# A third mixer whose keys, queries, values and gates load activations instead of weights, with norms, rotation and state output by token

## What is computed

```python
q, k, v, z, xbc, dt_raw = split(h @ w_in, [1024, 2048, 3072, 4096, 6144])   # h = rms_norm(x)
attn = dilated_attention(q, k, v, positions, g_q, g_k)     # 16 heads of 64
ssm = ssd_mixer(z, xbc, dt_raw, ...)                       # 16 heads of 64, state 128, 4 groups
x = x + concat(rms_norm(attn), ssm) @ w_out
```

## Time and profile before

| | us |
|---|---|
| median of three runs | 3288.57 (3285.89 to 3290.23) |
| profiled execution, its own time | 3288.93 |
| its span in the profile | 3287.0 |
| TensorE busy | 3270.5 (99%), 16658 matmuls |
| VectorE, ScalarE, POOL busy | 2215.1 (67%), 1524.6 (46%), 188.7 (6%) |
| third mixer, from its first weight matmul to its last state product | 2014.8 to 2369.7, 354.9 |

### The profile page before, as it was taken

The page is one execution under the profiler, slowest core; times in us unless marked ns, Lnnn a source line. Parts: engine busy times, 40 slices in busy tenths (PEclk is TensorE's granted clock), DMA queues, the critical chain, the costliest instruction groups (busy, mean ns, idle before and its releaser), DMA issues.

```text
span 3287.0 us, 41280 instructions
## 1 busy us (share of the span) xinstructions
PE 3270.5 (99%) x16658; PEld 2778.4 (85%) x16658; DVE 2215.1 (67%) x1898; ACT 1524.6 (46%) x1520; POOL 188.7 (6%) x272
## 2 busy tenths in 40 slices
PE   8999999999999999999999999999999999999999
PEld 7888888888888888888888888999989888888887
DVE  6565777777676665777777766577776566665565
ACT  6645434444445654444444345347554533333333
POOL 0100000000000000000000000001030000000000
PEclk9999999999999999999999999999999999999999
DMA  7456777777755446877777764434454455555554
GB/s 281 155 179 223 267 261 254 248 255 251 259 195 206 161 166 208 278 251 260 253 247 254 256 215 158 167 130 145 139 205 152 168 192 191 191 191 191 191 191 166
DMA packets 106523, 686.29 MB, mean 209 GB/s; under 512 B 14064, under 2 KB 16144, under 8 KB 29616
## 3 DMA queue, kind: packets, MB, share of 16 engines
q1 hardware_dynamic: 84128, 591.43, 50.3%
q0 software_dynamic: 22288, 93.31, 9.2%
HBM read 640.81 MB, written 2.10 MB: 196 GB/s over the span
## 4 chain that ended last, share of the span: by engine, by line
PE 99%; DVE 1%; DMA 1%; ACT 0%; issue 0%; DVEq 0%; POOL 0%
PE ps L540 24%; PE ps L542 24%; PE ps L541 24%; PE ps L520 7%; PE ps L498 4%; PE ps L522 3%; PE ps L499 3%; PE ps L500 3%; PE ps L562 1%; PE ps L645 0%; PE ps L634 0%; PE ps L690 0%; DMA gain_rows_sb<-in_gain_rows 0%; PE ps L604 0%; DVE w_lo L1785 0%; PE ps L911 0%
## 5 line engine op out<-in xcount | busy, mean ns | idle before, releaser
L1200 ACT ACTIVATE w_hi<-w_raw 128x2048 fp32r<-128x2048 f32 x558 | 1067.4, 1915 | 1198.5 <-DMA w_raw<-in_weights 1198.5
L1785 DVE TENSOR_TENSOR w_lo<-w_raw,w_hi 128x2048 fp32r<-128x2048 f32 x558 | 1275.0, 2292 | 484.3 <-ACT w_hi L1200 481.7
L540 PE MATMUL ps<-w_hi,actsb 128*128 128x512 f32 x1440 | 562.4, 391 | 0.0
L542 PE MATMUL ps<-w_lo,actsb 128*128 128x512 f32 x1440 | 560.4, 389 | 0.0
L541 PE MATMUL ps<-w_hi,actsb 128*128 128x512 f32 x1440 | 560.3, 389 | 0.0
L540 PE MATMUL ps<-w_hi,h_hi 128*128 128x512 f32 x1216 | 473.7, 390 | 0.0
L541 PE MATMUL ps<-w_hi,h_lo 128*128 128x512 f32 x1216 | 473.3, 389 | 0.0
L542 PE MATMUL ps<-w_lo,h_hi 128*128 128x512 f32 x1216 | 473.1, 389 | 0.0
L542 PEld LDWEIGHTS ps<-w_lo,actsb 128*128 128x128 f32 x1440 | 270.4, 188 | 56.1
L541 PEld LDWEIGHTS ps<-w_hi,actsb 128*128 128x128 f32 x1440 | 270.5, 188 | 55.2
L540 PEld LDWEIGHTS ps<-w_hi,actsb 128*128 128x128 f32 x1440 | 270.4, 188 | 55.1
(11 more groups left out here) (388 smaller groups left out, 3799.6 us busy)
## 6 DMA issues: line engine op xcount, KB each, us to landing
w_raw<-in_weights SPq DMA_DIRECT2D x558, 1024.0 KB, 4.8
gate_rows<-in_conv_rows POOLq DMA_DIRECT2D x20, 1024.0 KB, 5.0
up_rows<-in_conv_rows POOLq DMA_DIRECT2D x20, 1024.0 KB, 9.1
gate_prev<-gate_tokens POOLq DMA_DIRECT2D x20, 508.0 KB, 5.6
gate_next<-gate_tokens POOLq DMA_DIRECT2D x20, 508.0 KB, 6.8
up_prev<-up_tokens POOLq DMA_DIRECT2D x20, 508.0 KB, 5.7
up_next<-up_tokens POOLq DMA_DIRECT2D x20, 508.0 KB, 6.8
w_raw<-in_weights SPq DMA_DIRECT2D x4, 512.0 KB, 8.1
```

The lines of the kernel that those rows point to most:

```text
L540: mm(o, a_hi, hi, start=first and c == 0, stop=False)
L542: end = mm(o, a_hi, lo, start=False, stop=last and c == 3)
L1200: A(w_hi[:, s], w_raw[:, s], ACT.Identity).then_inc(hi_done, 1)
L1785: tt(w_lo[:, s], w_raw[:, s], hi_of(w_hi[:, s]), ALU.subtract).then_inc(w_ready, 1)
```

## The change

All in the third mixer and at the kernel's start.

- Keys, queries, values and z go to the token form, in the order k0, q0, k1, q1, v0, v1 (groups of four pieces), xbc wide as before, z0, z1. ScalarE copies each group out of PSUM with the norm factor, and for keys and queries squares it too. 32 of the 48 pieces change form.
- The norm and the rotation of keys and queries are done by token on VectorE, the rotation on the 16 rotated features of each head alone; TensorE then transposes each group to features (`qk_turned2`) and ScalarE copies it out with the unrotated gains. The sums, the rotation and the spread by matmul are gone; so are the value transposes.
- Scores, softmax and head products leave out the keys of the second half for the queries of the first, which the mask excludes.
- The state products have the decay matrix as stationary operand and the inputs, 64 columns, moving; y is then tokens by features, is multiplied by z, squared and scaled by token, and turned to features by 16 transposes in the output stage. Skip and gate are done by token too.
- The attention steps move earlier (scores at 13, 15, 24, 26 instead of 21, 23, 29, 31).
- Start of the kernel: `rising_clock`, seven matmuls on a tile of zeros, before the first piece; the first three pieces in `first_tokens`, which goes through hi x hi, hi x lo (w_lo) and lo x hi in turn; the first gains asked for by ScalarE's queue; positions asked for at the start.

```diff
-            opening(P_IN2, W_IN2, A0, S_OUT2, lambda: x_quarter(3, S_OUT2, A0 + 8))
-            factor_row(0)
-            wide(P_IN2 + 3, W_IN2 + 3, 3, A_IN)
-            dt_products()
-            for m in range(4, IN2):
-                piece2(m)
+            for m in range(IN2):
+                g, q = m // 4, m % 4
+                if XBC2 <= m < Z2:
...
+                    wide(P_IN2 + m, W_IN2 + m - XBC2, q, A_IN)
+                else:
+                    if g == 0:
+                        if q == 0:
+                            pe.wait_ge(added, S_OUT2 - 1)
+                        pe.wait_ge(act_ready, A0 + 4 * q + 4)
+                    elif q == 0:
+                        if g == 1:
+                            pe.wait_ge(added, S_OUT2)
+                        elif m < XBC2:
+                            pe.wait_ge(mix_copied, g - 1)
+                        else:
+                            pe.wait_ge(acc_free, W_KV + 2 * (g % 2) + 2)
+                    tokens(P_IN2 + m, q, A_IN, 4 * q, 2 * (g % 2), q == 0, q == 3)
+                if m == 0:
+                    x_quarter(3, S_OUT2, A0 + 8)
+                steps(m)
```

```diff
+            def rising_clock():
+                pe.wait_ge(zeros_ready, 1)
+                for _ in range(7):
+                    last = mm(ps[:, 7, 0:T], tmp[:, 0:P], tmp[:], start=True, stop=True)
+                last.then_inc(clock_up, 1)
+                pe.wait_ge(clock_up, 1)
+            def by_pass(p, bank, chunks, ready):
+                for term in range(3):
+                    for c in chunks:
+                        if term == 0:
+                            if c == chunks[0]:
+                                pe.wait_ge(*ready[0])
+                            pe.wait_ge(act_hi_done, 4 * p + c + 1)
+                        elif term == 1 and c == chunks[0]:
+                            pe.wait_ge(*ready[1])
+                        elif term == 2:
+                            pe.wait_ge(act_ready, 4 * p + c + 1)
+                        a = (act_hi, act_hi, act_lo)[term]
+                        w = (w_hi, w_lo, w_hi)[term]
+                        for b in range(TB):
+                            last = mm(ps[:, bank + b, :], a[...], w[...], ...)
```

```diff
-                for j in range(4):
-                    last = mm(ps[:, 4 + j, :], rot_g2[:, 1 - part], proj[:, c0 + 2 * j:c0 + 2 * j + 2], start=True, stop=True)
+            def qk_turned2(g):
+                pe.wait_ge(heads_roped, LAYERS * 3 + g + 1)
...
+                turned(6 - 2 * (g % 2), qk_tok[g], 0).then_inc(qk_turned, 1)
...
-                        last = mm(ps[:, 4 + i, b * T:(b + 1) * T], proj[half, Q2 + h // 2, b * P:(b + 1) * P],
-                                  proj[half, K2 + h // 2], start=True, stop=True)
+                        last = mm(ps[:, 4 + i, keys_of(b, True)], proj[half, Q2 + h // 2, b * P:(b + 1) * P],
+                                  proj[half, K2 + h // 2, 0:(b + 1) * P], start=True, stop=True)
...
-                        last = mm(o, vt2[:, kb, h * 64:(h + 1) * 64], pt2[:, kb, i],
+                        last = mm(o[:, kb * P:T], vt2[:, kb, h * 64:(h + 1) * 64], pt2[:, kb, i, kb * P:T],
...
-                    mm(o, xdt[:, 0, h * 64:(h + 1) * 64], dec[:, g % 2, i, 0:T], start=True, stop=False)
-                    last = mm(o[:, P:T], xdt[:, 1, h * 64:(h + 1) * 64], dec[:, g % 2, i, T:T + P],
-                              start=False, stop=True)
+                    mm(first, dec[:, g % 2, i, 0:P], inputs[0], start=True, stop=True)
+                    mm(second, dec[:, g % 2, i, P:T], inputs[0], start=True, stop=False)
+                    last = mm(second, dec[:, g % 2, i, T:T + P], inputs[1], start=False, stop=True)
...
-                if j == 0:
-                    per_head(S0 + 4, ps[0:16, 4, 0:T], sq_y, 8, per_row=2)
-                elif j == 1:
-                    pe.wait_ge(rows_ready, 2)
-                    pe.wait_ge(skipped, 4)
-                    spread(dtf, 6, range(4))
+                if j == 1:
+                    pe.wait_ge(mixed_ready, 1)
+                    turned(4, yt, 0)
+                    turned(6, yt, 1).then_inc(sgu_turned, 1)
```

ScalarE's and VectorE's new work, in brief:

```diff
+            def group_copied(g):
+                act.wait_ge(acc_done, P_IN2 + 4 * g + 4)
...
+                    if g < 4:
+                        A(qk_sq[g % 2][:, b], src, ACT.Square, scale=r_x[:, b:b + 1])
+                    last = A(dst, src, ACT.Identity, scale=r_x[:, b:b + 1])
+                last.then_inc(mix_copied, 1)
...
+            for g in range(SSM_GROUPS):
+                act.wait_ge(y_done, g // 2 + 1)
+                for b in range(TB):
+                    last = A(zt[:, b, 256 * g:256 * (g + 1)], yt[...], ACT.Square, accum_out=kf2[...])
+            last.then_inc(y_squared, 1)
...
+            def qk_rotated(g):
+                tt(rot_a[:], heads[:, :, :, 0:16], cos, ALU.mult)
+                tt(rot_b[:, :, :, 0:8], heads[:, :, :, 8:16], sin[:, :, :, 0:8], ALU.mult)
+                step(tt(rot_b[:, :, :, 8:16], heads[:, :, :, 0:8], sin[:, :, :, 8:16], ALU.mult))
+                last = tt(heads[:, :, :, 0:16], rot_a[:], rot_b[:], ALU.add)
...
+            y = yt[:].rearrange("p a (g d) -> p (a g) d", d=256)
+            tt(y, y, y_factor[:, :, None].to_broadcast([P, 8, 256]), ALU.mult).then_inc(mixed_ready, 1)
```

## The result

The changed kernel takes 3261.05 us (median of four runs, 3258.40 to 3262.15) against 3288.68 (3285.89 to 3290.23): ratio 0.9916, 95% interval 0.9903 to 0.9928. That is 27.6 us less, where 37.2 were forecast. The profiled execution has a span of 3260.1 us and a time of its own of 3261.95. TensorE still has nearly all of the chain of waits.

What follows compares the result with a forecast made beforehand. TensorE, with 99% of the chain of waits, was taken to bound the kernel. Savings and added costs on its queue summed to -37.2 us, so 3288.9 became 3251.7 us; the range was 3245 to 3266.

Steps and rivals of the forecast that it cites:

- Token pieces: Q, K, V and z weight pieces: 5.44 us each instead of 5.76, 10.2 us less over 32 pieces.
- the four turns: Transposing queries and keys to features in the mixer: four steps of 8 transposes, 0.8 us each, 3.2 us more.
- state products: End of mixer: 2.6 us a group instead of 1.5, 4.5 us more; bounds 0 and +9.6.
- the causal quarter: Mixer attention: skipping masked keys shortens scores, head products and transposes, 5.1 us less; bounds 1.7 and 5.6.
- the output stage: After the state products: per-head sums and a spread go, 16 transposes of y come; 3.8 us less.
- the opening: Kernel start: earlier first matmuls, piece 4 starting near 31.9 and a later wait gone; 2.1 us less.
- No fall stands near piece 16: Sign that the forecast is right: no stretch of clock 0.50 near piece 16 of the mixer.
- Nothing there ends last as long as each step is done a piece or two ahead: Mixer: ScalarE (at most 204 us busy) and VectorE (under 243.4) would not delay TensorE in a 324 us stage.
- The rival: New waits: an attention step late behind ScalarE's bunched work near pieces 14 to 20, 2.2 us a pass; 3258 to 3270, chance 0.14.
- The clock: Rival: short state-product matmuls drop the clock one to three times, 3.4 us each; with dearer products 3255 to 3266, chance 0.14.
- the sums of squares: Mixer: the matmul step for the norms of queries and keys disappears, 10.4 us less.
- The chain to y: Output stage: squares, root and scaling of y finish within 22 us of the state products, about 2 us to spare.

Runs made afterwards that it cites:

- e4_both: Changed kernel with the third bunch's head products one piece later and two decay-row spreads moved to mid-pieces 45 and 46; 3251.02 us.
- after: The changed kernel as first measured, against the kernel without the change; 3261.05 us, ratio 0.9916.
- e3_columns: Changed kernel with only the state products put back to their old form (64 columns stationary, 256 decay columns moving); 3250.40 us.
- before: The kernel without the change, the one the changed kernel is compared with; 3288.68 us.
- e9_products_twice: e4_both with the state products of groups 2 and 3 computed twice; 3256.38 us.
- e2_apart: Changed kernel with the decay-row spreads for groups 2 and 3 moved from right behind state products to the middle of pieces 45 and 46; 3255.95 us.
- e6: e4_both with the opening's pieces in their old forms and no warming matmuls, the gains still through ScalarE's queue; 3254.05 us.
- e10_turned_thrice: e4_both with the 16 transposes of y made three times, 48 on end; 3254.97 us.
- after_again: The changed kernel run again unedited, on another chip; 3259.19 us.
- e11_spreads_thrice: e4_both with the decay-row spreads of groups 0 and 1 made three times on end; 3264.74 us.
- e7_no_warming: e4_both without the seven warming matmuls on zeros at the start, the new order of products kept; 3252.08 us.

## Why the prediction was right and wrong

- **The sum over TensorE's own work was right**, term by term: stage -31.3 forecast, -31.4 in e4_both (323.4 against 354.9). Token pieces are 5.44 apart (and 0.1 more at the first behind a step), the four turns 0.79 each, state products +4.3 (forecast 4.5), the causal quarter -5.1, the output stage -3.7 in after and -4.1 in e4_both (forecast -3.8), the opening -2.0 to -2.9 (forecast -2.1). No fall stands near piece 16 in any of the changed kernels.
- **The state products' price** came from the sums by token, 0.10 a record, over the bound by columns: 0.11 a record in the trace. A group takes 2.60 us in e4_both and 1.50 in e3_columns, 1.7 times less.
- **The step that failed first** is "Nothing there ends last as long as each step is done a piece or two ahead": one step did, the copy of the third bunch, at 3.3 us. I took it from ScalarE's total (forecast 204 us, measured 196.6), looked for a bunch around pieces 14 to 20, and did not set the order of ScalarE's calls beside that of before, where it stands in the diff that exponentials moved ahead of a copy. The rival had the mechanism (ScalarE's queue), though not its place, and gave it 2.2 us a pass.
- **The clock** was a rival too (one to three falls by short matmuls, 3.4 each), at 0.14 with the state products; the sum put it at nothing. It came three times, some 8 us in that execution: twice by the state products, as the rival had it, and once inside the wait, which no rival had. The argument against it, that these products have 64 columns, was right as far as it went, since 5.3 us of products alone don't bring it down (e9_products_twice); what I left out is that the spread, 1.9 us with 16 rows, follows on the now longer products. And the 10.4 us that I took off for the sums of squares hold the fall of before, 6.7 us at 0.50, worth 3.4 by an estimate (half of it). I took it for a fixed part of before; by the mean clocks it was in most of its runs, not in all.
- **The chain to y** ends in time: y is scaled by 2366.6 and the transposes start at 2368.35, 1.8 us later; I had counted 2.
- Both misses made it 3261 rather than 3252. That is outside the band of the sum (3246 to 3257) and inside the range only because the range had been stretched for these two rivals; that both came and still fell short of 3266 is partly luck.

## What to carry to other kernels

Sum TensorE's edits from start-to-start distances and they hold to a few tenths; then write out each supplying engine's queue between a step and the step that uses it, in the new order, since its share of busy time shows no bunch. Try to put a step one piece later before making its supplier faster: here that took back 3.3 us and cost nothing. And look at what stands on end between weight pieces: here, with half a piece between the 16-row spreads and the state products, the clock stood at 1.00 around them in all seven traces of it (e2, e4, e6 to e10), where the four with the same products and spreads on end had six falls.

## What the runs showed of the hardware

- The granted clock fell inside a 3.3 us wait of TensorE in two of four profiled executions that had it (after and after_again, not e2_apart and e3_columns), near that place in none of the nine that had not, and at no wait of 1.9 us or less once the clock was up. The runs of the changed kernel lose some 3 to 8 us by falls (3257.7 to 3262.5, less 3251.0 and 3.3 for the wait), which is most of the scatter of its runs (4.8 us for after_again, 0.5 for e4_both, whose clock stays up).
- The granted clock also fell to 0.50 in steps in which the profile shows TensorE busy without a gap: 24 records of 16 rows and 256 columns on end (5.6 us) had a fall in both places of e11_spreads_thrice, 3.4 us at 2294.3 and 10.2 us at 2304.6. 48 records of 64 columns over 128 rows (5.3 us, twice in e9_products_twice), and 48 transposes (5.2 us, e10_turned_thrice), had none.
- With seven fp32 matmuls on zeros the granted clock is up at 5.1 us from the start in after (4.0 to 7.4 in the eleven kernels that have them), without them at 12.0 in e7_no_warming and 14.1 in before, where the first matmuls stand 0.43 us apart and later ones of the same shape 0.23. The kernel won nothing by it that the traces show: it then stands 0.8 us for w_lo before piece 4.
